# The normed tile that the expert dots read goes into the two PSUM banks of the V sums

## The reference

```python
hid = jax.nn.gelu(jnp.einsum('td,thkd->thk', x_blk, u_tab[idx_blk]), approximate=False)
coef = (g_blk * hid.astype(jnp.float32)).astype(x_blk.dtype)
return jnp.einsum('thk,thkd->td', coef, v_tab[idx_blk])
```

## Time and profile before

| | |
|---|---|
| time, median of 3 runs | 4173.53 us (4168.82 to 4189.53) |
| span of the profiled execution, first to last instruction | 4065.6 us |
| VectorE busy | 2832.9 us (70%) |
| GpSimd busy | 2533.7 us (62%) |
| TensorE busy | 2484.2 us (61%) |
| ScalarE busy | 670.3 us (16%) |
| read from HBM | 1280.42 MB, 318 GB/s over the span |

### The profile page before, as it was taken

The page is one execution under the profiler, slowest core; times in us unless marked ns, Lnnn a source line. Parts: engine busy times, 40 slices in busy tenths (PEclk is TensorE's granted clock), DMA queues, the critical chain, the costliest instruction groups (busy, mean ns, idle before and its releaser), DMA issues.

```text
span 4065.6 us, 29120 instructions
## 1 busy us (share of the span) xinstructions
PE 2484.2 (61%) x7326; PEld 1341.5 (33%) x7326; DVE 2832.9 (70%) x5396; ACT 670.3 (16%) x1466; POOL 2533.7 (62%) x2067
## 2 busy tenths in 40 slices
PE   6654458795686147877487335869468523873057
PEld 3432333343343133333333223334334222331023
DVE  2437885669848986567965797477974798567863
ACT  2310111111211102112121101121121111110011
POOL 0005686467745887366873787547774688747776
PEclk8776768896798558988588656989679756886589
DMA  8146999899997889889898889969999888978999
GB/s 283 56 141 263 346 314 388 295 356 359 339 389 278 289 307 357 326 296 400 302 374 319 286 299 353 386 245 377 346 338 376 287 294 310 377 290 287 365 409 356
DMA packets 400926, 1296.79 MB, mean 319 GB/s; under 512 B 38174, under 2 KB 82724, under 8 KB 397932
## 3 DMA queue, kind: packets, MB, share of 16 engines
q0 software_dynamic: 294912, 1073.87, 72.2%
q1 hardware_dynamic: 97772, 183.35, 12.4%
q10 hardware_dynamic: 8064, 37.58, 2.3%
HBM read 1280.42 MB, written 14.23 MB: 318 GB/s over the span
## 4 chain that ended last, share of the span: by engine, by line
PE 29%; DVE 22%; POOL 19%; issue 15%; DMA 9%; ACT 3%; DVEq 1%; SPq 0%; ACTq 0%; PEldq 0%; POOLq 0%; PEld 0%
POOL ring L370 19%; PE acc L686 13%; PE work L699 11%; DVE ring L950 4%; DMA wring<-in_peer_wq 4%; DMA wring<-in_w_in 3%; DVE proj L975 3%; DVE proj L971 2%; DVE hbuf L963 2%; PE work L672 2%; DMA ring<-in_peer_v,idxU 1%; ACT arena L400 1%; DMA ring<-in_peer_u,idxU 1%; PE work L819 1%; PE work L663 1%
## 5 line engine op out<-in xcount | busy, mean ns | idle before, releaser
L370 POOL DMA_INDIRECT ring<-in_peer_u,idxU x1024 | 1410.4, 1377 | 781.4 <-issue 355.4
L686 PE MATMUL acc<-ring,diag 128*128 128x512 f32 x2240 | 1084.7, 644 | 526.1 <-ACT diag L421 495.5
L370 POOL DMA_INDIRECT ring<-in_peer_v,idxU x896 | 951.7, 1062 | 665.3 <-DVE hbuf L963 258.0
L950 DVE CUSTOM_DVE_ANT_0 ring<-ring,n2U 128x1024 f32<-128x1024 f32 x1024 | 1203.3, 1222 | 105.0 <-DMA ring<-in_peer_u,idxU 94.4
L686 PEld LDWEIGHTS acc<-ring,diag 128*128 128x128 f32 x2240 | 457.4, 207 | 1145.8 <-issue 947.2
L963 DVE SCALAR_TENSOR_TENSOR hbuf<-ring,coefV,hbuf 128x1024 f32 (+1 forms) x464 | 596.3, 1285 | 260.2 <-DMA ring<-in_peer_v,idxU 176.0
L699 PE MATMUL work<-wring,nT 128*128 128x512 f32 (+1 forms) x1408 | 640.7, 609 | 80.8 <-DMA wring<-in_w_in 40.2
L699 PEld LDWEIGHTS work<-wring,nT 128*128 128x128 f32 x1408 | 279.8, 203 | 420.9 <-issue 336.4
L421 ACT ACTIVATE diag<-ident,coefV 128x128 f32<-128x128 f32 x560 | 184.5, 391 | 675.3 <-PE acc L686 521.6
L672 PE MATMUL work<-arena 128*128 128x128 f32 x768 | 144.2, 357 | 219.8 <-issue 205.5
L971 DVE MAX8 proj<-proj 128x8 f32<-128x128 f32 x256 | 51.0, 278 | 300.5 <-ACT proj L400 300.5
(11 more groups left out here) (219 smaller groups left out, 2065.6 us busy)
## 6 DMA issues: line engine op xcount, KB each, us to landing
wring<-in_w_in SPq DMA_DIRECT2D x80, 898.0 KB, 14.4
wring<-in_peer_wq SPq DMA_DIRECT2D x64, 1024.0 KB, 15.6
wring<-in_w_out SPq DMA_DIRECT2D x32, 1024.0 KB, 17.8
ring<-in_peer_u,idxU POOLq DMA_INDIRECT x1024, 6.3
ring<-in_peer_v,idxU POOLq DMA_INDIRECT x896, 6.4
par<-par_scr ACTq DMA_DIRECT2D x8, 1184.0 KB, 7.0
arena<-keys_scr ACTq DMA_DIRECT2D x8, 1024.0 KB, 8.3
proj<-proj_scr ACTq DMA_DIRECT2D x3, 1796.0 KB, 10.8
```

Of the source, the lines that this page charges most:

```text
L370: nc.gpsimd.indirect_dma_start(ring[:, s * D:(s + 1) * D], None, table, bass.IndirectOffsetOnAxis(ap=idx, axis=0)).then_inc(row_in[s], 16)
L686: ins = nc.tensor.matmul(acc[c][:], diag[:, d * P:(d + 1) * P], ring[:, s * D + 512 * c:s * D + 512 * c + 512], start=(m == 0 and r == 0), ...
L950: V.tensor_tensor_reduce(out=rw, in0=rw, in1=n2U[:], scale=1.0, scalar=0.0, op0=ALU.mult, op1=ALU.add, accum_out=hid[:, kk:kk + 1]).then_i ...
```

## The change

`acc[0]` and `acc[1]` become the two halves of one PSUM tensor `accs` of 128 by 1024, which fills the same two banks. After `sums_in` (or alone, in the first step with dots) VectorE copies `n2U` there (`place_n2`), and the dots read it there in place of `n2U`. `sums_in` adds the two banks in one instruction of 1024 columns in place of two of 512. The copies at the end of a step, the places of all units and all waits of GpSimd, TensorE and ScalarE stay.

```diff
-        acc = [ctx.enter_context(nc.psum_tensor(f"acc{b}", [P, 512], f32)) for b in range(2)]
+        accs = ctx.enter_context(nc.psum_tensor("accs", [P, D], f32))
+        acc = [accs[:, 512 * c:512 * c + 512] for c in range(2)]
...
-                    V.tensor_tensor_reduce(out=rw, in0=rw, in1=n2U[:], scale=1.0, scalar=0.0, op0=ALU.mult, op1=ALU.add,
+                    V.tensor_tensor_reduce(out=rw, in0=rw, in1=accs[:], scale=1.0, scalar=0.0, op0=ALU.mult, op1=ALU.add,
                                            accum_out=hid[:, kk:kk + 1]).then_inc(usedU, 1)
...
-                    if u and not first and b == 0:
-                        sums_in(j)
+                    if u and b == 0:
+                        if not first:
+                            sums_in(j)
+                        place_n2()
...
-                for i in range(2):
-                    hh = hbuf[:, bass.ds(((t - 2) % TILES) * D + 512 * i, 512)]
-                    link(V.tensor_tensor(hh, hh, acc[i][:], ALU.add), "acc_read" if i else "dve_chain")
+                hh = cut(hbuf, D, (t - 2) % TILES)
+                link(V.tensor_tensor(hh, hh, accs[:], ALU.add), "acc_read")
+
+            def place_n2():
+
+                link(V.tensor_copy(accs[:], n2U[:]))
...
                     mix("last_n")
                     sums_in(t)
+                    place_n2()
                     mix("last_u")
```

## The result

The runs came from several chips, and this case can't be read without that: on five of them the kernel before took 4051 to 4061 us, on two occasions (perhaps one chip twice) 4164 to 4171 us. I call the first kind ordinary and the other the slow chip. The times printed ahead of the prediction are from the slow chip. The profile printed with them, with its 4065.6 us, is of the ordinary kind, so the 108 us "beside the span" there are no time at the ends of an execution but the distance between two kinds of chip. The ratios are worked out over all executions and need not be the quotient of the medians beside them.

A forecast was written before the change was run, and what follows sets the result against it. It took GpSimd's gathers, held up by VectorE's dots, as the bound, VectorE a few per cent behind. 28.8 + 19.6 + 23.5 + 7 - 9.8 + 1.2 - 5 = 65.3 us, so 4108 us from 4173.5 (chance 0.58), range 4050 to 4152.

The forecast's parts named there:

- Two SBUF inputs of VectorE hold the gather up and one does not: U gathers beside dots: up to 1.99 us should fall to 0.94 once dots read one input from PSUM.
- follow steps: Three steps: 9.6 us of waits for rows go in each, 28.8 us gained, with VectorE late next.
- the tail: Last 128 dots, no mixer: 185 us at 354 GB/s, 23.5 us of waits for rows gained, DMA late next.
- The term for solo and lead steps: Four steps: faster gathers fill 20 us running at 306 of 407 GB/s, 4.9 us each, 19.6 us gained.
- the first V rows: After the dots: with gathers ahead these rows are already there, an estimated 7 us gained over seven steps.
- With the 108 us around it: Added to the predicted span of 4000 us, from the median of 4173.5, to give a time of 4108 us.
- TensorE, ScalarE and SyncE run what they ran: Other engines: unchanged, with no wait added for the two PSUM banks and no term in the sum.
- L1022 or the projection's weights come later by what the rows gave: Sign that the prediction is wrong: the add after the mixer's convolution, or the weights, late by the rows' gain.
- The rows ahead of them are the same in number: Projection's weights in solo and lead steps: the ring holds 16 rows either way, so equally many precede them.
- If the cover fails ... up to all of it comes back: Follow steps: if the mixer's own waits on TensorE grow, up to all of the 28.8 us is lost.
- The slower one: Rival, chance 0.05: a second input from PSUM lengthens each dot; at +0.20 us a dot, 4245 us.
- less arrives: Rival, chance 0.16: waits turn into waits on the mixer; gain 24 us, 4150 us at worst, some 4135 otherwise.

The follow-up runs named there:

- e2_copy_only: The changed kernel with the copies into PSUM and the merged sum, but dots reading the normed tile from SBUF as before; ordinary chip: 4052.3 us (0.9979).
- e13_hybrid: Changed kernel, but dots of solo and lead steps read the normed tile from SBUF; follow steps and tail from PSUM; ordinary chip, no load: 3991.4 us (0.9854).
- e3_after: The changed kernel once more, unchanged, on ordinary chip 14: 3986.6 us, ratio 0.9828 to the kernel before.
- e1_before: The kernel before once more, unchanged, on an ordinary chip: 4065.6 us, ratio 0.9996.
- both loads: Added to either kernel: 512 HBM-to-HBM copies spread over all DMA engines plus 512 of 12 KB on one engine; slow chip: 4322.9 us before, 4385.6 us changed.
- e18_before_both: The kernel before plus 512 spread copies and 512 copies of 12 KB on one DMA engine, slow chip: 4322.9 us (1.0365).
- e19_after_both: The changed kernel plus 512 spread copies and 512 copies of 12 KB on one DMA engine, slow chip: 4385.6 us (1.0508).
- the 37 KB load: 512 HBM-to-HBM copies of 37 KB, made for one DMA engine, added to a kernel: 4291.9 us before, 4250.4 us changed, 4264.4 us with SBUF reads in solo and lead.

## Why the prediction was wrong, and where right

- **The gathers, the dots, the copies: right.** 998 and 996 ns (950 to 1000 predicted), 1217 ns a dot, the copy 1.23 us. "Two SBUF inputs of VectorE hold the gather up and one does not" held in every run: e2_copy_only, with the copies but SBUF reads, gained nothing that its interval can tell, and its gathers stayed at 1344 ns. The Trainium skill, "SBUF — State Buffer", section Who interferes with whom, infers that descriptor generation isn't stalled by an instruction that takes only the shared read interface; these gathers contradict that inference. The larger fixed part for a PSUM source in the Trainium skill, "VectorE: DVE Perf Modes", section on the TRN2 errata, doesn't show for this instruction: 1217 ns from PSUM, 1224 from SBUF on chip 14.
- **The sum: right on ordinary chips, in part by luck.** On chip 14 follow steps gave 28 us (28.8 predicted), solo and lead 20 (19.6), the tail 22 (23.5), together 70 from windows that sum to 1771 and 1701. The medians gave 56 to 72 for 65.3. Follow steps and tail are the mechanism predicted. The term for solo and lead steps agrees by luck: e2_copy_only has 17 of the 20 us with its gathers still held up, and e13_hybrid loses nothing by reading SBUF there, so 20 x (1 - 306/407) was no gain of faster gathers. It is made up outside the stretches, where the sum had next to nothing (7 for the first V rows, less 8.6 for copies and `sums_in`) and e3_after is 15 us shorter than e1_before.
- **"With the 108 us around it": wrong.** 4065.6 and 4173.5 us were the same kernel on two kinds of chip, not a span and its surroundings; the forecast for its own execution, 4000 us, is within 14 us of all four ordinary medians. Setting it beside the other chip's median carried an effect from one kind of chip to the other.
- **"TensorE, ScalarE and SyncE run what they ran": the step that failed on the slow chip.** The prediction gave these three no term. They do run the same instructions, but not at the same times: SyncE issued 22 weight tiles 1 to 28.5 us after their slot was free, ScalarE began 11 copies late by 104 us in all, and TensorE stood 41.6 us before projection products for nothing recorded (7.0 in e3_after). With both loads, where the kernel before stands beside it, TensorE's unexplained idle time before the convolution's input is 38 us in place of 1 and makes most of the 47 us by which that input comes later. Solo and lead steps, put at -19.6 us with 0 as the worst end, cost +68 there, and follow steps, put at -28.8, cost +31 (both e18_before_both to e19_after_both). The last part of the prediction had named this sign ("L1022 or the projection's weights come later by what the rows gave"), but no rival carried its price. "The rows ahead of them are the same in number" isn't refuted: TensorE's waits for weights in these pieces are 31 us with and without the change.
- **"If the cover fails ... up to all of it comes back": too small.** Follow steps lost their row waits (33.7 us left in all stretches) and got the mixer's chain instead, 99.3 us at L1130 in eight waits on the slow chip against 14.9 in e1_before; it comes back more than in full, for late reports weren't in any row that I had.
- **The rivals.** The slower one was placed in the dot, which was the wrong place; "less arrives", waits that turn into waits on the mixer, was the right mechanism with the wrong end: 0 as its limit, where +54 was measured.

What makes the slow chip slow, and why its reports come late, stays open. That the change brings more of them rests on one trace of the kernel before (no late weight issue, 8 late copies) and two of the changed kernel, and the first of these is loaded. In solo and lead stretches 47 of the +68 us come before the convolution's input, mostly as TensorE's pauses; how the rest and the +31 us of follow steps divide wasn't measured beyond the late copies named.

## What to carry to other kernels

Before a span is set against a median, ask whether both are from one chip: a gap of 2.7% with nothing recorded around the span was the hint. When a wait grows, follow it engine by engine, down to the semaphore, before it is put down to bandwidth: here the DMA engines looked at fault, but TensorE's waits for weights had not grown, and a slot free at 1869.48 us had been reported at 1890.84. A copy alone as a control, and a hybrid, can take a term away that the sum seemed to confirm, as with the 19.6 us of solo and lead steps. Where the freed speed buys nothing (solo and lead steps of an unloaded ordinary chip, by e13_hybrid; under the 37 KB load it bought 14 us) it can be left out, though whether that saves the slow chip wasn't run.

## What I had not expected

Chips differ in more than rate: 410 against 375 GB/s in the tail, and reports of finished matmuls that come up to 28 us late on one kind, and in none of 17 traces on the other. And a load that takes 12% more DMA traffic from every engine damped the gain only from 56 to 43 us.
